# Seven products instead of eight in the first slab of nine gate-and-up groups, with the groups alternating between two sets of PSUM banks

## The reference, cut to what matters

```python
h = rmsnorm(x, norm_ffn_pre)                       # 256 x 2048
m = (silu(h @ w_ffn_gate) * (h @ w_ffn_up)) @ w_ffn_down
x = x + rmsnorm(m, norm_ffn_post)                  # w_gate, w_up: 2048 x 5632
```

## Time and profile before

| what | value |
|---|---|
| median of 3 runs | 2452.81 us (2452.26 to 2452.99) |
| the profiled execution | 2453.34 us, of which the span from first to last instruction is 2451.5 us |
| mean granted TensorE clock | 0.996 of full speed |
| PE, weight loads, DVE, ACT busy | 98%, 82%, 73%, 50% of the span |

### The profile page before, as it was taken

The page is one execution under the profiler, slowest core; times in us unless marked ns, Lnnn a source line. Parts: engine busy times, 40 slices in busy tenths (PEclk is TensorE's granted clock), DMA queues, the critical chain, the costliest instruction groups (busy, mean ns, idle before and its releaser), DMA issues.

```text
span 2451.5 us, 28699 instructions
## 1 busy us (share of the span) xinstructions
PE 2408.9 (98%) x11138; PEld 1998.8 (82%) x11138; DVE 1799.5 (73%) x2366; ACT 1223.0 (50%) x1587; POOL 99.2 (4%) x150
## 2 busy tenths in 40 slices
PE   5999999999999999999999999999999999999998
PEld 4888888888788888888888888888888888888887
DVE  6998988766776675767777678965776766758776
ACT  4757665445544444444444544544544444445443
POOL 1210000000000000000000212000000000000000
PEclk8999999999999999999999999999999999999999
DMA  9997655564565566555656655445555565565654
GB/s 383 357 384 248 244 190 171 183 251 150 175 198 194 189 193 199 191 189 182 231 187 208 197 189 193 168 148 196 182 196 189 192 198 194 189 195 182 223 189 155
DMA packets 189495, 507.06 MB, mean 207 GB/s; under 512 B 17792, under 2 KB 18080, under 8 KB 188080
## 3 DMA queue, kind: packets, MB, share of 16 engines
q1 hardware_dynamic: 177008, 456.92, 55.3%
q0 software_dynamic: 11824, 46.14, 5.1%
q10 hardware_dynamic: 528, 2.16, 0.2%
HBM read 503.06 MB, written 2.10 MB: 206 GB/s over the span
## 4 chain that ended last, share of the span: by engine, by line
PE 95%; DVE 3%; DMA 1%; ACT 0%; issue 0%; SPq 0%; DVEq 0%; ACTq 0%
PE acc L677 29%; PE acc L679 29%; PE acc L678 29%; PE wk L1119 1%; PE wk L1118 1%; PE wk L1120 1%; DVE gate L1798 1%; PE wk L703 1%; DMA raw<-in_ada_w 1%; DMA raw<-in_w_in 1%; PE acc L1119 1%; PE acc L1118 1%; PE acc L1120 1%; DVE lo L1823 0%; PE wk L1190 0%
## 5 line engine op out<-in xcount | busy, mean ns | idle before, releaser
L677 PE MATMUL acc<-hi,h 128*128 128x512 f32 x2592 | 1017.3, 392 | 2.1 <-ACT proj L1384 0.7
L679 PE MATMUL acc<-hi,h 128*128 128x512 f32 x2592 | 1009.6, 389 | 0.0
L678 PE MATMUL acc<-lo,h 128*128 128x512 f32 x2592 | 1009.0, 389 | 0.0
L1823 DVE SCALAR_TENSOR_TENSOR lo<-raw,gcols,hi 128x1024 fp32r<-128x1024 f32 (+1 forms) x464 | 569.1, 1270 | 184.1 <-ACT hi L1269 181.5
L1269 ACT ACTIVATE hi<-raw,gcols 128x1024 fp32r<-128x1024 f32 (+1 forms) x464 | 497.4, 1128 | 380.7 <-PE acc L679 315.5
L1821 DVE TENSOR_TENSOR lo<-raw,hi 128x1024 fp32r<-128x1024 f32 (+2 forms) x428 | 486.7, 1187 | 121.8 <-ACT hi L1269 120.2
L677 PEld LDWEIGHTS acc<-hi,h 128*128 128x128 f32 x2592 | 486.9, 188 | 104.6 <-issue 3.7
L679 PEld LDWEIGHTS acc<-hi,h 128*128 128x128 f32 x2592 | 486.6, 188 | 102.2
L678 PEld LDWEIGHTS acc<-lo,h 128*128 128x128 f32 x2592 | 486.9, 188 | 99.1
L1269 ACT ACTIVATE hi<-raw 128x1024 fp32r<-128x1024 f32 (+2 forms) x428 | 413.5, 1026 | 275.1 <-DMA raw<-in_w_ffn_down 114.8
L677 PE MATMUL acc<-hi,g_hi 128*128 128x512 f32 x544 | 211.9, 390 | 0.0
(11 more groups left out here) (369 smaller groups left out, 1589.6 us busy)
## 6 DMA issues: line engine op xcount, KB each, us to landing
raw<-in_w_ffn_gate SPq DMA_DIRECT2D x176, 512.0 KB, 3.8
raw<-in_w_ffn_up SPq DMA_DIRECT2D x176, 512.0 KB, 4.6
raw<-in_w_ffn_down SPq DMA_DIRECT2D x176, 512.0 KB, 5.0
raw<-in_w_in SPq DMA_DIRECT2D x144, 512.0 KB, 4.8
raw<-in_w_kv SPq DMA_DIRECT2D x64, 512.0 KB, 4.8
ada_raw<-in_ada_w POOLq DMA_DIRECT2D x38, 512.0 KB, 7.7
gate_raw<-in_ada_w POOLq DMA_DIRECT2D x32, 512.0 KB, 6.3
raw<-in_w_out SPq DMA_DIRECT2D x32, 512.0 KB, 5.1
```

Of the source, the lines that this page charges most:

```text
L677: pe.matmul(o, l_hi, w_hi[:, c], start=first, stop=False, skip_group_check=loaded)
L678: pe.matmul(o, l_hi, w_lo[:, c], start=False, stop=False, skip_group_check=loaded)
L679: mm = pe.matmul(o, l_lo, w_hi[:, c], start=False, stop=last, skip_group_check=loaded)
L1823: ins = vec.scalar_tensor_tensor(out=lo[:, r, c], in0=raw[:, r, c], scalar=gcols[:, st.gain, k:k + 1], in1=hi[:, m % HI_SLOTS, c], op0=ALU ...
```

## The change

For groups 2 to 10 of gate-and-up (`CHAINED = 2`, nine groups in each of two layers), slab 0 is done in seven products, with a "sums" slab behind it. The last slab of the group before is woven in between them. Even groups fill `acc`, odd groups fill `wk`. The products of slab 0 aren't kept apart: they run through the banks in a chain, in which a bank is copied or subtracted while PE works on others. PE's order for group g, with x0 to x3 its banks, is this (the number of matmuls in brackets; P7 is slab 7 of group g-1, whose four bank parts are of 6 matmuls each; B, T and S are weight blocks, sums of them, and sums of activations):

1. x0 = A11*B11 [3]; P7 bank 0 [6]; x3 = S1*T1 [3]; P7 bank 1 [6];
2. ACT has copied x0 to x2 (`chain_start`); x2 += S2*T2 [3]; P7 banks 2 and 3 [12]; x0 += A12*B21 [3];
3. ACT has copied x2 to `part_sums[0]` (`chain_copy 0`); x2 += S3*(B12+B22) [3]; slab 1 into x0 [6];
4. DVE has made x1 = x3 - `part_sums[0]` (`chain_end 0`); x1 += S4*B22 [3]; slab 1 into x1 [6];
5. ACT has copied x2 to `part_sums[1]` (`chain_copy 1`); x2 += A22*T4 [3]; slab 1 into x2 [6];
6. DVE has made x3 = x3 - `part_sums[1]` (`chain_end 1`); slab 1 into x3 [6]; then slabs 2 to 6 as before.

`chain_end 1` stands on DVE behind the first four block transposes, and ahead of the conversion of slab 2. The weight slab and the sums carry no gain here, so once in each layer, in group 1, DVE and ACT multiply the gain into the first two row blocks of the activations, in place, and make S1 to S4 (`gu_side_sums`, `gu_side_hi`, `gu_side_lo`). Some semaphores are merged to make room; their meaning stays. The core of the diff:

```diff
-                if st in st_down and s in SEVEN[g]:
+                if st in st_down and s in SEVEN[g] or st in st_gu and g >= CHAINED and s == 0:
                     slabs.append((st, g, f"sums{s}"))
...
+    def bank(st, g, b):
+        return (wk if st in st_gu and g % 2 else acc)[:, b, :]
...
+        def gu_seven(l, g):
...
+            pe.wait_ge(slab_split, m + 1)
+            pe.wait_ge(side_made, GU_SIDES[l] + 3)
+            pe.wait_ge(acc_free[0], use[st.name, g, 0] - 1)
+            add(x0, h(0, 0), m, 0, True, True).then_inc(chain_made, 1)
+            before(0, 0)
+            pe.wait_ge(slab_split, m + 2)
+            pe.wait_ge(acc_free[3], use[st.name, g, 3] - 1)
+            add(x3, s1, m + 1, 0, True, True)
+            before(0, 1)
+            pe.wait_ge(acc_loaded[2], gu_loaded(l, g, 2))
+            add(x2, s2, m + 1, 1, read=True).then_inc(chain_made, 1)
+            before(1, 0)
+            before(1, 1)
+            add(x0, h(1, 0), m, 2)
+            pe.wait_ge(chain_copied, 2 * i + 1)
+            add(x2, s3, m, 1, read=True).then_inc(chain_made, 1)
+            pe.wait_ge(slab_split, m + 3)
+            gu_part(l, g, 1, 0, 0)
+            pe.wait_ge(acc_loaded[1], gu_loaded(l, g, 1))
+            add(x1, s4, m, 3).then_inc(slab_used, 1)
+            gu_part(l, g, 1, 0, 1)
+            pe.wait_ge(chain_copied, 2 * i + 2)
+            add(x2, h(1, 1), m + 1, 2).then_inc(slab_used, 1)
+            gu_part(l, g, 1, 1, 0)
+            pe.wait_ge(acc_loaded[3], gu_loaded(l, g, 3))
+            gu_part(l, g, 1, 1, 1)
...
-            for g in range(FG - 1):
-                for s in range(2 if g else 3, st.slabs):
+            for s in range(3, st.slabs):
+                product(st, 0, s)
+            for g in range(1, CHAINED):
+                for s in range(st.slabs - (g == CHAINED - 1)):
                     product(st, g, s)
...
+            for g in range(CHAINED, FG):
+                gu_seven(l, g)
+                for s in range(2, st.slabs - (g < FG - 1)):
+                    gu_product(l, g, s)
...
+        def chain_start(l, g):
+            act.wait_ge(chain_made, 3 * gu_no(l, g) + 1)
+            act.activation(bank(st, g, 2), bank(st, g, 0), ACT.Copy).then_inc(acc_loaded[2], 1)
+        def chain_copy(l, g, i):
+            act.wait_ge(chain_made, 3 * gu_no(l, g) + i + 2)
+            act.activation(part_sums[:, i, :], bank(st_gu[l], g, 2), ACT.Copy).then_inc(chain_copied, 1)
...
             def evac(g):
+                if CHAINED <= g + 1 < FG:
+                    chain_start(l, g + 1)
+                    conv_to(number[st.name, g + 1, 1])
                 if g:
                     act.wait_ge(g_blocks, (FG - 1) * l + g)
                 for t in range(TT):
+                    if t and CHAINED <= g + 1 < FG:
+                        chain_copy(l, g + 1, 0)
                     bank_wait(act, st, g, t, 0)
...
                 evac(g)
-                conv_to(end + (6 if g < FG - 1 else 4))
+                if CHAINED <= g + 1 < FG:
+                    conv_to(end + 4)
+                    chain_copy(l, g + 1, 1)
+                conv_to(end + ((7 if g + 1 >= CHAINED else 6) if g < FG - 1 else 4))
                 post(g)
...
+        def chain_end(l, g, i):
+            b = 3 if i else 1
+            vec.wait_ge(chain_copied, 2 * gu_no(l, g) + i + 1)
+            vec.tensor_tensor(bank(st, g, b), bank(st, g, 3), part_sums[:, i, :], ALU.subtract).then_inc(acc_loaded[b], 1)
...
             def evac(g):
+                if CHAINED <= g + 1 < FG:
+                    conv_to(number[st.name, g + 1, 1])
                 for t in range(TT):
+                    if t and CHAINED <= g + 1 < FG:
+                        chain_end(l, g + 1, 0)
...
                         turn_blocks(g, f)
-                        conv_to(end + 3 + f)
+                        if f == 0 and g + 1 >= CHAINED:
+                            chain_end(l, g + 1, 1)
+                        conv_to(end + (4 if g + 1 >= CHAINED else 3) + f)
```

More of the change, by code:

```diff
@@ L320, in sevens, with followed_by_sums, gain_of, sums_before @@
         return st_down.index(st) if st in st_down and s in SEVEN[g] else None
+    def followed_by_sums(m):
+        return m + 1 < N_SLABS and is_sums(m + 1)
+    def gain_of(m):
+        return None if is_sums(m) or followed_by_sums(m) else slabs[m][0].gain
+    def sums_before(m):
+        return 2 * sum(is_sums(i) for i in range(m))
+    def gu_no(l, g):
+        return (FG - CHAINED) * l + g - CHAINED
+    N_SIDES = len(SEVEN[0])
+    DOWN_SIDES = [3 + l * (3 + 2 * N_SIDES) for l in range(2)]
+    GU_SIDES = [l * (3 + 2 * N_SIDES) for l in range(2)]
+    DOWN_HIS = [2 + l * (2 + N_SIDES) for l in range(2)]
+    GU_HIS = [l * (2 + N_SIDES) for l in range(2)]
     LANDED, landings = [], [0] + [32] * (RING - 1)
@@ L660, in product @@
                         pe.wait_ge(acc_free[b], use[st.name, g, b])
-                    o = acc[:, b, 0:st.width]
+                    o = bank(st, g, b)[:, 0:st.width]
                     for kk in range(st.kt):
@@ L1133, in seven, with gu_part @@
             add(acc[:, 2, :], gt(k1, 1), m + 1, 2).then_inc(slab_used, 1)
+        def gu_part(l, g, s, t, n):
+            st = st_gu[l]
+            m, b = number[st.name, g, s], st.bank(t, n)
+            o = bank(st, g, b)
+            for kk in range(st.kt):
+                k, a = st.k(s, kk), (kk * st.halves + n) * HALF
+                w_hi, w_lo = hi[:, m % HI_SLOTS, a:a + HALF], lo[:, place(m) % RING, a:a + HALF]
+                l_hi, l_lo = h(k, t)
+                last = s == st.slabs - 1 and kk == st.kt - 1
+                pe.matmul(o, l_hi, w_hi, start=False, stop=False, skip_group_check=g >= CHAINED)
+                pe.matmul(o, l_hi, w_lo, start=False, stop=False, skip_group_check=g >= CHAINED)
+                mm = pe.matmul(o, l_lo, w_hi, start=False, stop=last, skip_group_check=g >= CHAINED)
+            if (t, n) == (TT - 1, 1):
+                mm.then_inc(slab_used, 1)
+            elif last:
+                mm.then_inc(acc_done[b], 1)
@@ new lines, in gu_product, with add @@
+        def gu_product(l, g, s):
+            pe.wait_ge(slab_split, number[st_gu[l].name, g, s] + 1)
+            for t in range(TT):
+                for n in range(2):
+                    gu_part(l, g, s, t, n)
+        def gu_seven(l, g):
+            st, i = st_gu[l], gu_no(l, g)
+            m = number[st.name, g, 0]
+            x0, x1, x2, x3 = (bank(st, g, b) for b in range(4))
+            s1, s2, s3, s4 = ((gu_side_r[:, 0, j, :], gu_side_r[:, 1, j, :]) for j in range(4))
+            before = lambda t, n: gu_part(l, g - 1, st.slabs - 1, t, n)
+            def add(o, lhs, slab, q, first=False, read=False):
+                c = slice(q * HALF, (q + 1) * HALF)
+                w_hi, w_lo = hi[:, slab % HI_SLOTS, c], lo[:, place(slab) % RING, c]
+                pe.matmul(o, lhs[0], w_hi, start=first, stop=False, skip_group_check=True)
+                pe.matmul(o, lhs[0], w_lo, start=False, stop=False, skip_group_check=True)
+                return pe.matmul(o, lhs[1], w_hi, start=False, stop=read, skip_group_check=True)
+            pe.wait_ge(slab_split, m + 1)
[24 more added lines that the diff above has]
+            gu_part(l, g, 1, 1, 1)
@@ L1814, in conv @@
             w = cols_of(m) // n
-            if sevens(m) is not None:
-                vec.wait_ge(sums_made, 2 * sum(is_sums(i) for i in range(m)) + 2)
+            if followed_by_sums(m):
+                vec.wait_ge(sums_made, sums_before(m) + 2)
             for kk in range(n):
@@ L2721, in _ @@
         pool.wait_ge(diff_in, 16 * 7)
[L2722 removed]
+        for buf, st in ((kv, st_k), (q2, st_q)):
             for g in range(2):
```

108 lines of the change are left out of this document (77 added, 31 removed).

## The result

| | before | changed |
|---|---|---|
| median of 4 runs | 2452.9 us (2452.26 to 2453.11) | 2440.53 us (2439.1 to 2441.12) |
| profiled execution, span | 2453.34, 2451.5 us | 2440.28, 2438.5 us |

The ratio is 0.9949, with a 95% interval of 0.9932 to 0.9966. In two further sets of five runs (e8 and e11) the changed kernel took 2440.20 and 2440.04 us.

What follows compares the result with a forecast made beforehand. The prediction took gap-free PE in gate-and-up as the bound: 2453.34 - 12.24 for 54 matmuls + 0 for covered waits and hidden work = 2441.1 us profiled, 2440.6 in runs, range 2439.8 to 2444.5.

Steps and rivals of the forecast that it cites:

- Bound: Gate-and-up of both layers: PE has no gap in 400 us, so time only goes away as matmuls, 0.2267 us each.
- Part 1: Slab 0 of nine groups in two layers: 54 matmuls go, 12.24 us saved, all on the path.
- Part 2: Six new PE waits on ACT and DVE at each of 18 boundaries: all covered, least margins 1.6 and 1.7 us.
- Cost of the place: DVE at each boundary: `chain_end 1` behind four transposes costs nothing, its input being ready only at 10.6 us.
- Part 3: Work added per group: DVE 6.0 us, to 35.4 of 42.8 (83%), ACT to 23.2; both hidden, 108 us if uncovered.
- Part 4: Slots and transfers at boundaries: landing takes at most 5.5 us, slab 2's hi starts at 7.74, other slabs arrive in time.
- Part 5: Preparation once a layer in group 1: 4.1 us on DVE, 1.3 on ACT, hidden; 11 us without cover.
- A: Boundaries: every new wait is covered, 2440.6 us (2440.0 to 2441.5); chance 0.86.
- D: Gate-and-up: a matmul left out gives back less than its distance; 2446.7 us with half given back; chance 0.02.
- B: Each boundary: one link slightly late, PE waits 0.2 to 0.4 us, times 18; 2444 to 2448 us; chance 0.07.
- C: Boundaries: slab 2's transfer lands late, stopping PE; slower than before, 2462 us with landings of 10.5; chance 0.02.
- E: Gate-and-up: the seven run but groups get no shorter, the next slab being paced by transfers; 2452.8 us; chance 0.01.

Runs made afterwards that it cites:

- e8: The changed kernel run again without a further edit, in a further set of five runs: 2440.20 us.
- e11: The changed kernel once more without a further edit, in a set of five runs, for comparison with e10 and e9: 2440.04 us.
- e1: Changed kernel with the first product of every seven issued twice, 54 matmuls more, all waits and copies kept: 2452.33 us, ratio to before 0.9999.
- e2: Changed kernel with CHAINED = 7 in place of 2, so eight sevens instead of eighteen: 2447.31 us, ratio to before 0.9978.
- e5: Changed kernel with ACT making the same copy two times more ahead of `chain_copy 1`: 2439.93 us, ratio to before 0.9948.
- e6: Changed kernel with ACT making the same copy five times more ahead of `chain_copy 1`: 2467.68 us, ratio to before 1.006.
- e3: Changed kernel with `chain_end 1` on DVE moved ahead of the first four block transposes: 2442.15 us, ratio to before 0.9955.
- e10: The edit of e3 run again, beside the changed kernel on the same chip: 2441.69 us, against 2440.04 for the changed kernel.
- e4: Changed kernel with `chain_end 1` on DVE moved behind the second four block transposes and slab 2's conversion: 2462.43 us, ratio to before 1.004.
- e9: Changed kernel with CHAINED = 1, two sevens more and the preparation in group 0; group 1's output wrong, time only: 2441.43 us, ratio to before 0.9956.

## Why the prediction was right, point by point

- **Bound.** PE without a gap in both layers' gate-and-up was the right ground: e1 gives and takes 12 us with the 54 matmuls alone.
- **Part 1, the matmuls.** 12.24 us forecast. Measured: 12.4 by medians, 6.11 and 6.13 us in the two layers' traces. The group distance came out at 42.84, as worked out. By the Trainium skill, "TensorE: Matmul & The Clock Gate", section "Back-to-back issue gap", it would have been 7.1 us, an estimate from its 131 ns; e1 and e2 disagree with it and decide for the distance of 0.2267 us in this kernel.
- **Part 2, the waits.** No wait of PE or of a weight load in 18 boundaries. The ACT and DVE rows that follow lie within 0.5 us of the times that were laid out (in brackets), none of them later: `chain_start` 0.87 (0.94), `chain_copy 0` 4.96 (5.02), slab 2's hi 7.74 (7.74), `chain_copy 1` 9.83 (10.0), `chain_end 1` 10.44 (10.7), slab 2's lo to 13.5 (14.0). The unknown copy from PSUM to PSUM took 0.58 (0.60 taken). The forecast margins of 1.6 and 1.7 are 1.8 and 2.1: two instructions that follow each other on ACT or DVE overlap by some 0.1 us in their rows (a lo of two is 2.47 and not 2.58), which I had left out. But both are counted to the matmul, and the wait is met by its weight load 0.23 us before: so 1.6 and 1.9. That the forecast's 1.6 and 1.7 are near these is in part luck: two errors of about the same size in opposite directions. e5 and e6 bear the first margin out, e3 and e10 the second.
- **Cost of the place.** "Placing `chain_end 1` behind four transposes costs nothing" held; ahead of them it costs 0.8 us by the traces (e3, e10), behind eight it costs 22 us (e4). I had not priced either.
- **Part 3, DVE at 83%.** In the group from 803.63 to 846.47 DVE is busy for 34.8 us (35.4 laid out), 81%, and ACT for 22.7 (23.2). Both are hidden. The slab that must be used ahead of the sums is slab 4 of the old group and not slab 3, as `weight_sums` waits for it; the time given, -10.9, is that of slab 4.
- **Part 4, transfers: the step that was off.** I bounded a landing by 5.5 us, the highest of the earlier trace rows. The changed kernel's rows for `raw` say otherwise, where the transfers of four slabs now follow each other closely, behind each boundary:

```profile
DMA to landing us min/median/max: 3.5/4.6/8.0
```

  The same view for 840 to 850 us, ahead of the boundary's releases, and for 850 to 860, where slabs are issued at 850.69, 854.09, 856.13 and 858.85:

```profile
DMA to landing us min/median/max: 3.8/4.2/4.6
...
DMA to landing us min/median/max: 3.7/5.0/7.3
```

  e2 has both kinds of group in one execution. The same view for 700 to 930 us, with groups of eight products, and for 935 to 1095, with sevens:

```profile
DMA to landing us min/median/max: 3.6/4.3/5.2
...
DMA to landing us min/median/max: 3.6/4.6/7.5
```

  It cost nothing, since the bunched transfers belong to slabs 3 and later, whose margins were some 3 us and more, and the transfer of slab 2 is issued ahead of the bunch. But a bound taken from evenly spaced transfers isn't one for bunched ones.
- **Part 5, the preparation.** Hidden: e2's line through zero, for group 1 and for group 6. In group 0 it isn't (e9). The scaling of 128x256 columns took 0.35 us each, where I took 0.42.
- **Rivals.** A, as forecast. D falls with e1, B with e1 and e5. C is real as a mechanism, with e4 and e6 as its two forms; a transfer was not what brought it about. E falls with the group distance.

## What to carry to other kernels

Where an engine has no gap at all over a stage, each of its instructions is worth its distance from start to start, and a new dependence on another engine is worth nothing up to a margin and one for one beyond it: so lay out one period with durations and the measured lag between engines, write down for each new wait when it is met and when it is wanted, and count the margin to the first instruction behind the wait, which for a matmul is its weight load (0.23 us earlier here). On an engine that works in strict order the place of one instruction is part of the design: moved behind four more block transposes and a slab's conversion, one subtraction made this kernel lose 22 us. A preparation that is free in one group needn't be so in the one before; look at what that engine does there.

## What the runs showed of the hardware that I had not expected

- A stop of PE costs more than the idle time named in its row. In e4 the row says 0.95 us; the distance to the matmul before is 1.33 instead of 0.23, and the matmul after it starts 0.34 behind instead of 0.23. Together 1.22 us at each boundary, and the group distance is 44.08, 1.24 more than 42.84; 18 of them are 22.3 us, and the medians show 21.9. In e6 it is 1.21 named and 1.51 paid. The idle time is counted from the end of a row of 0.39 us, where the next matmul would have started after 0.23; this is 0.16 of the difference, and the late second matmul 0.11.
- A wait can cost time without a line among PE's waits: in e3 and e10 only the weight load shows it (0.3 us, once), with a group distance of 43.09 instead of 42.87.
- Transfers of 512 KB landed up to 8.0 us after their issue where pairs of them followed each other by 2 to 3.4 us, against up to 5.5 us (layer 0) and 5.7 (layer 1) where a pair came every 5.4 us. That the bunching is the cause is borne out by e2, where the highest is 5.2 in groups without sevens and 7.5 in those with them; what slows the transfers isn't shown. In gate-and-up of layer 0, every stretch of 10 us with a landing above 6 us lies behind a boundary, as 850 to 860 us does.
- The time until the first gate-and-up group ends differs by more than a microsecond between executions of kernels that are the same there: 672.54, 673.68, 673.85 and 672.26 us (changed, e11, e3, e10). In the three traces of the changed kernel (spans 2438.5, 2438.4 and 2439.6 us; first group's end 672.54, 672.49 and 673.68) that is the whole difference. Where in the beginning it arises was not looked at.
